# One group of the long convolution's input 512 columns wide, its halves joined by a transfer

## The reference

```python
    n = _rmsnorm(h, norm_mix_g[l])
    z = n @ w_in[l]
    c_a, c_g, q, k, v, qi, ki, wi, gc_logit, ga_logit = _split_cols(z, IN_SIZES)
...
def _conformer_conv(a, gate, conv_w, conv_b, ln_g, ln_b, w_out):
    u = a * jax.nn.sigmoid(gate)
    u = lax.conv_general_dilated(
        u, conv_w[:, None, :].astype(u.dtype), window_strides=(1,),
        padding=[(CONV_WIDTH_2 - 1, 0)], dimension_numbers=('NWC', 'WIO', 'NWC'),
        feature_group_count=CONV_CH) + conv_b
    u = jax.nn.silu(_layernorm(u, ln_g, ln_b))
    return u @ w_out
```

## Time and profile before

| | before |
|---|---|
| time, median of 3 runs | 909.94 us (909.59 to 910.15) |
| the profiled execution's own time | 909.86 us |
| its span, first to last instruction | 908.0 us |
| granted TensorE clock over the span, as a share of full speed | 0.998 |
| TensorE busy | 901.4 us, 99% |
| VectorE busy | 678.3 us, 75% |
| ScalarE busy | 573.5 us, 63% |
| chain that ended last | TensorE 98%, DMA 1%, VectorE 1% |

### The profile page before, as it was taken

The page is one execution under the profiler, slowest core; times in us unless marked ns, Lnnn a source line. Parts: engine busy times, 40 slices in busy tenths (PEclk is TensorE's granted clock), DMA queues, the critical chain, the costliest instruction groups (busy, mean ns, idle before and its releaser), DMA issues.

```text
span 908.0 us, 13440 instructions
## 1 busy us (share of the span) xinstructions
PE 901.4 (99%) x4933; PEld 768.9 (85%) x4933; DVE 678.3 (75%) x1181; ACT 573.5 (63%) x1017; POOL 46.6 (5%) x55
## 2 busy tenths in 40 slices
PE   9999999999999999999999999999999999999997
PEld 7888877788888888888898998888788888888886
DVE  5868798378776666667699999997786776666665
ACT  6667878745654455446678779865946764554444
POOL 0300000000000000000012122100000000000000
PEclk9999999999999999999999999999999999999999
DMA  9967665565565556554599999975475356555551
GB/s 333 313 179 207 165 186 162 188 227 186 165 189 194 196 194 202 192 199 154 190 244 276 270 268 277 232 223 196 141 245 169 116 166 227 188 185 186 186 186 47
DMA packets 94848, 182.67 MB, mean 201 GB/s; under 512 B 7936, under 2 KB 13120, under 8 KB 94528
## 3 DMA queue, kind: packets, MB, share of 16 engines
q1 hardware_dynamic: 88944, 165.30, 55.4%
q0 software_dynamic: 5472, 15.99, 9.8%
q10 hardware_dynamic: 368, 0.52, 0.2%
HBM read 164.69 MB, written 1.05 MB: 183 GB/s over the span
## 4 chain that ended last, share of the span: by engine, by line
PE 98%; DMA 1%; DVE 1%; SPq 0%; ACT 0%; issue 0%; DVEq 0%
PE pb L456 95%; PE pb L460 3%; DMA raw<-in_w_first 1%; SPq L397 0%; SPq L400 0%; DVE XT L2222 0%; DVE wlo L2233 0%; DVE wlo L1666 0%; ACT whi L1058 0%; DVE XS L2480 0%; ACT XT L1058 0%; DVE XS L2487 0%; DVEq L56 0%; ACT MSQ L1638 0%; PE pb L851 0%
## 5 line engine op out<-in xcount | busy, mean ns | idle before, releaser
L1666 DVE TENSOR_TENSOR wlo<-raw,whi 128x1024 fp32r<-128x1024 f32 (+1 forms) x298 | 353.8, 1213 | 113.0 <-ACT whi L1058 112.6
L1058 ACT ACTIVATE whi<-raw 128x1024 fp32r<-128x1024 f32 (+1 forms) x304 | 309.3, 1039 | 131.4 <-PE pb L456 111.5
L456 PE MATMUL pb<-XT,whi 128*128 128x512 f32 (+2 forms) x1208 | 294.2, 362 | 0.1
L456 PE MATMUL pb<-whi,ZO 128*128 128x512 f32 (+1 forms) x808 | 251.8, 389 | 0.0
L456 PEld LDWEIGHTS pb<-XT,whi 128*128 128x128 f32 (+1 forms) x1208 | 204.2, 189 | 23.9 <-issue 1.2
L456 PE MATMUL pb<-XT,wlo 128*128 128x256 f32 (+1 forms) x1032 | 183.5, 282 | 0.0
L456 PEld LDWEIGHTS pb<-whi,ZO 128*128 128x128 f32 x808 | 151.3, 188 | 31.5 <-DVE wlo L1666 1.1
L456 PEld LDWEIGHTS pb<-XT,wlo 128*128 128x128 f32 (+1 forms) x1032 | 161.3, 190 | 14.8
L456 PE MATMUL pb<-whi,XT 128*128 128x512 f32 (+1 forms) x544 | 170.9, 390 | 0.7 <-ACT whi L1058 0.5
L456 PE MATMUL pb<-wlo,ZO 128*128 128x512 f32 (+1 forms) x404 | 156.6, 388 | 0.0
L456 PEld LDWEIGHTS pb<-whi,XT 128*128 128x128 f32 x544 | 101.0, 188 | 22.7 <-ACT whi L1058 2.1
(11 more groups left out here) (262 smaller groups left out, 649.6 us busy)
## 6 DMA issues: line engine op xcount, KB each, us to landing
raw<-in_w_in SPq DMA_DIRECT2D x105, 512.0 KB, 5.0
raw<-in_w_ff SPq DMA_DIRECT2D x64, 512.0 KB, 5.2
raw<-in_w_up SPq DMA_DIRECT2D x32, 512.0 KB, 4.5
raw<-in_w_down SPq DMA_DIRECT2D x32, 512.0 KB, 4.9
YC<-PRODS POOLq DMA_DIRECT2D x16, 384.0 KB, 7.1
PRODS<-PRODS POOLq DMA_DIRECT2D x14, 384.0 KB, 7.2
raw<-in_w_branch_b SPq DMA_DIRECT2D x8, 512.0 KB, 5.3
raw<-in_w_out SPq DMA_DIRECT2D x8, 512.0 KB, 3.9
```

The source lines that it names most:

```text
L456: return e.matmul(o, l, r, start=start, stop=stop, skip_group_check=True)
L1058: return e.activation(o, i, ACT.Copy, scale=scale)
L1666: e.tensor_tensor(wlo[u % NW][:, 0:c], raw[u % NRAW][:, 0:c], whi[u % NW][:, 0:c].bitcast(F32), ALU.subtract).then_inc(lo, 1)
```

## The change

`b2_ca1` becomes a name of `JOINED`: TensorE computes it with `cols_pair`, ScalarE copies the halves of its four tiles to HQ when the gates have been read from it (`gs_made`, 8), and POOL issues a join for it, ahead of tap 5. `conv_in1` becomes a side of VectorE's run of `b2_qi`: it waits for the join in the third unit and multiplies from HQ. ScalarE waits for these products (`halves_in`, 8) before it copies the halves of `b2_qi` to the same HQ. In `TAPS` one tap moves: 3, 5 in place of 4, 4 in the second and third unit of `b2_qi`.

```diff
-TAPS = (0,) + (4,) * 6 + (0,) + (4,) * 3 + (6, 6) + (4,) * 5 + (4, 3) * 3 + (3,) + (1,) * 9 + (3,) * 18
+TAPS = (0,) + (4,) * 6 + (0, 4, 3, 5, 6, 6) + (4,) * 5 + (4, 3) * 3 + (3,) + (1,) * 9 + (3,) * 18
...
-JOINED = ("b1_x0", "b1_c1", "b1_x1", "b1_b0", "b1_b1", "mk", "b2_cg1", "b2_qi")
+JOINED = ("b1_x0", "b1_c1", "b1_x1", "b1_b0", "b1_b1", "mk", "b2_cg1", "b2_ca1", "b2_qi")
...
             run("b2_ca1", conv_gate1(), products)
+            e.wait_ge(gs_made, 8)
+            copy_halves("b2_ca1")
             run("b2_qi", products)
+            e.wait_ge(halves_in, 8)
             copy_halves("b2_qi")
...
-                                e.wait_ge(*(out_at["b2_ca1", f - 4] if f >= 4 else (halves_in, f + 1)))
+                                e.wait_ge(halves_in, f + 1)
...
             def conv_in1():
+                yield
+                yield
+                e.wait_ge(joined["b2_ca1"], 16)
                 for f in range(4):
                     e.wait_ge(gs_made, 4 + f + 1)
-                    col_product("b2_ca1", f, U2[:, 4 + f, 30:286], GS[:, f, :])
+                    e.tensor_tensor(U2[:, 4 + f, 30:286], HQ[:, 0, f, :], GS[:, f, :], ALU.mult).then_inc(halves_in, 1)
+                yield
...
             run("b2_ca1", taps)
-            conv_in1()
-            run("b2_qi", taps)
+            run("b2_qi", conv_in1(), taps)
...
                 for k in range(2, 31):
+                    if k == 5:
+                        join("b2_ca1")
                     e.wait_ge(prod_made, k + 1)
```

## The result

| | before | after |
|---|---|---|
| time, median of 5 runs | 909.94 us (909.59 to 910.15) | 914.37 us (911.94 to 915.24) |
| the profiled execution's own time, its span | 909.86, 908.0 us | 915.24, 913.3 us |
| granted TensorE clock over the span | 0.998 | 0.996 |

The kernel became slower by 0.45%: the ratio of the mean times is 1.0045, with an interval from 1.0031 to 1.0059. The spread has grown too: 3.3 us between the five runs, where it was 0.6 us. The profiled run is the slowest of the five. They stand in the order of their clock: 911.94 us at 0.999, 913.75 at 0.998, 914.37 and 914.47 at 0.997, 915.24 at 0.996.

A forecast was written before the change was run, and what follows sets the result against it. TensorE was taken to bound the kernel, on the ending chain for 98% of the span. 909.86 us plus 2.7 us for b2_ki's later start, with the 0.59 us saving already inside, gave 912.6 us; range 909.2 to 914.9.

The forecast's parts named there:

- The matmuls: b2_ca1 on TensorE, 512 columns wide, would take 11.16 instead of 11.75 us, saving 0.59 us on the path.
- the rival without a gain: b2_ca1's matmuls do not become quicker at 512 columns; it would add 0.4 us; no chance of its own given.
- The issue: POOL would issue b2_ca1's join at 471.6 us, behind a tap transfer, although its data lie ready at 469.35.
- The latency: b2_ca1's join would land 9.0 us after its issue, at 480.6; ends for the range 5.1 and 11.3 us.
- The wait: VectorE idle some 4 us before the products; TensorE waits 3.3 us, so b2_ki starts at 483.1, 2.7 us later.
- The covers: After b2_ki, spare time at b2_qi's join, low parts, weight loads and biased scores absorbs later delays: nothing, at worst 1.0 us.
- The full queue: Rival: b2_ca1's join queues fully behind the tap transfer, 11.3 us; TensorE 5.0 us late, 914.9 us; chance 0.19.
- The hidden transfer: Rival: b2_ca1's join lands within 6.3 us of issue; below 5.7 only the saving remains, 909.3 us; chance 0.17.

The follow-up runs named there:

- the repeat: The changed kernel run once more without any edit, beside the kernel before: 913.25 us, ratio 1.0041.
- TensorE kept busy: The changed kernel plus 24 matmuls whose result nobody reads, between b2_qi and b2_ki: 912.46 us, ratio 1.0032.
- the buffer of its own: The changed kernel with b2_ca1's halves in a separate buffer HA, so ScalarE waits neither for gates nor products; POOL's order unchanged: 912.21 us, ratio 1.0026.
- the early join: The changed kernel with POOL issuing b2_ca1's join ahead of tap 4 instead of tap 5, HQ still shared: 909.41 us, ratio 1.0001.
- extra_transfer: The kernel before plus one accumulating 512 KB SBUF transfer behind tap 4, for which nothing waits in this stretch: 909.79 us, ratio 1.0000.

## Why the prediction was right in its mechanism, and what it left out

- **The matmuls.** `b2_ca1` takes 468.65 - 457.49 = 11.16 us, as forecast; the rival without a gain is out.
- **The issue.** Forecast 471.6, measured 471.62, 0.54 us behind tap 4 (471.08 for 471.09).
- **The latency.** Forecast 9.0 us between 5.1 and 11.3, measured 9.2 in the profiled run, 8.6 in the profile of the repeat, 9.2 with TensorE kept busy, 9.3 with the buffer of its own. The Trainium skill's estimate of 3.2 us (DMA: Bandwidth & Descriptors, section Anatomy of one DMA — SWDGE (gpsimd) path) is met by none of the joins here; even the early one took 6.8 us.
- **The wait.** VectorE idle 4.12 us (forecast some 4), `b2_ki` at 483.02 (483.1), TensorE's wait 3.05 us (3.3). From landing to `b2_ki` it took 483.02 - 480.82 = 2.20 us, 0.27 less than the 2.47 given to the products, one copy and three hand-overs. This term is **+2.65 us, forecast +2.7**.
- **What the sum left out.** The prediction let TensorE go on as before once it had its bank, so it put the clock behind the wait at nothing. TensorE went on at half its clock: 5.16 - 2.81 = 2.35 us in `b2_ki` and 0.25 in `mk`. 909.86 + 2.65 + 2.35 + 0.25 = 915.1 us; the profiled run took 915.24. The same sum for the profile of the repeat, 909.86 + 1.80 + 1.57 = 913.2 us, stands beside 913.44. The runs in which the clock hardly fell are near the forecast's 912.6: 911.94 us at 0.999, and 912.46 us in the median with TensorE kept busy.
- **The covers.** "At nothing" for the low parts and the biased scores holds in the changed kernel: the score there begins at 561.34 and TensorE needs it at 564.46, with 2.6 us to spare as before. But it holds only because TensorE is late too:

```profile
561.34 0.53 DVE L1813 SCALAR_TENSOR_TENSOR SM<-pb,SC 128x384 f32<-128x384 f32 x1
...
564.46 0.82 PE L456 MATMUL pb<-KT,QT 128*128 128x128 f32 x4
```

The buffer of its own takes TensorE's wait away, and VectorE's delay comes through, 912.21 - 909.6 = 2.6 us over the kernel before. One place was not named by the prediction: the low part of `mk`'s last unit, with 491.99 - 486.89 = 5.1 us of cover before. So the two bills are not added: where TensorE is late by the wait, the list shows no wait for VectorE, with the clock fallen (5.25 us late) or kept up (3.1 us late). Taking away TensorE's wait alone leaves 2.6 us of the loss, keeping its clock alone leaves 2.9 us (912.46 - 909.6). What is left when VectorE's delay alone goes was not tried.
- **The rivals.** The full queue (914.9 us) is nearest to the measured time, and for another reason: the join took 9.2 us, not 11.3. Who has only the time would have chosen the wrong one. The median of 914.37 us lies outside the forecast's own 911.7 to 913.6 us; that the wider range holds it is luck, since its upper end came from this rival. The hidden transfer (909.3 us) is what the early join makes true, at 909.41 us.

That the lower clock accounts for all of the distance from 912.6 to the median of 914.37 is not shown run by run: of the ten runs of the changed kernel two have a trace.

## What to carry to other kernels

A wait that stops the bounding engine can have a second price behind it, here 1.57 and 2.6 us in the two profiled runs: ask how fast that engine runs when it starts again. When two engines become late at one place, the bills need not add up, so test the removal of both together, and look at what each has left to spare further on. Issue a transfer whose data are ready ahead of one whose data are not: POOL issues in program order, and here the join landed after 6.8 and 7.9 us ahead of the tap transfer, after 8.6 to 9.3 us behind it.

## What the runs showed of the hardware

- After a standstill of 3.05 us TensorE ran at 0.50 of its clock for the following 5 us of full work; after one of 2.50 us it ran 0.4 us at 1.00 and then some 3 to 4 us at 0.50. Beside the waits of 0.9 and 1.0 us with the buffer of its own the windows show 1.00 throughout, as does this one:

```profile
560.00:570.00 10.00, 8.94 (x45) 7.09 (x44) 9.86 (x23) 9.54 (x25) 1.62 (x2) 1.00 1.04 279
```

- At half the clock `b2_ki` took 1.84 times as long, not twice (5.16 for 2.81 us). The first two matmuls after the standstill of 2.50 us took 0.43 us together, those after 3.05 us 0.67 us.
- The same accumulating transfer of 512 KB inside SBUF landed after 5.1 to 10.0 us, by its place among other transfers: 5.1 with nothing ahead of it on POOL, 6.8 and 7.9 early, 8.6 to 9.3 behind tap 4, 10.0 as the further transfer of extra_transfer.
